# Stage edges of a two-block transformer kernel: other bank pairs, later loads, an unrolled pass, sums on two engines, recurrence steps moved

## The reference, cut to what matters

```python
# first block
y = jnp.einsum('bsmc,mcd->bsmd', branches, w_branch)          # three branches
x = x + jnp.sum(sigmoid(merge_gate) * y, axis=2) @ w_out
h = rms_norm(x, norm_mlp)
x = x + jnp.square(jax.nn.relu(h @ w_mlp_in)) @ w_mlp_out     # 2048 -> 8192 -> 2048
x = rms_norm(x, norm_final)
# second block
h = rmsnorm(x, norm_mix)                                      # two norms, one behind the other
u, q_in, f_in, i_in, g_in = jnp.split(h @ w_in, splits, axis=-1)
# hgrn2_mixer: S_t = diag(f_t) S_{t-1} + (1 - f_t) outer i_t ; o_t = S_t^T q_t
q = silu(q_in)
log_f = log(lb + (1 - lb) * sigmoid(f_in)); k = 1 - exp(log_f)
o = rmsnorm(o, norm_gain) * silu(g_in)                        # norm per head
```

## Time and profile before

| | |
|---|---|
| median of 3 runs | 2823.69 us (2822.1 to 2824.51) |
| the profiled execution | 2825.74 us, its span 2824.2 us |
| PE busy | 2739.8 us, 97% of the span |
| DVE busy | 1437.3 us, 51% |
| ACT busy | 1166.0 us, 41% |
| mean granted TensorE clock | 0.997 of full speed |

### The profile page before, as it was taken

The page is one execution under the profiler, slowest core; times in us unless marked ns, Lnnn a source line. Parts: engine busy times, 40 slices in busy tenths (PEclk is TensorE's granted clock), DMA queues, the critical chain, the costliest instruction groups (busy, mean ns, idle before and its releaser), DMA issues.

```text
span 2824.2 us, 33252 instructions
## 1 busy us (share of the span) xinstructions
PE 2739.8 (97%) x12784; PEld 2077.4 (74%) x12784; DVE 1437.3 (51%) x1645; ACT 1166.0 (41%) x1520; POOL 12.9 (0%) x20
## 2 busy tenths in 40 slices
PE   8999999999999999999999999999999999999896
PEld 6888777778888888888888788888888785434342
DVE  4444455656655565555556744577654463312122
ACT  4443355653354444444444644455444441000001
POOL 0000000000000000000000000000000000000000
PEclk9999999999999999999999999999999999999999
DMA  6966845556656555555555476554555459999997
GB/s 244 329 215 211 300 155 171 180 198 242 214 180 230 186 193 188 185 191 192 186 186 179 171 278 212 191 190 171 209 189 188 158 185 371 426 427 426 427 427 323
DMA packets 115679, 672.57 MB, mean 238 GB/s; under 512 B 12125, under 2 KB 17677, under 8 KB 40688
## 3 DMA queue, kind: packets, MB, share of 16 engines
q1 hardware_dynamic: 86048, 612.52, 59.2%
q10 hardware_dynamic: 27264, 46.58, 4.6%
q0 software_dynamic: 2256, 11.95, 1.2%
HBM read 647.37 MB, written 28.35 MB: 239 GB/s over the span
## 4 chain that ended last, share of the span: by engine, by line
PE 85%; DMA 6%; DVE 4%; ACT 2%; issue 1%; DVEq 1%; ACTq 0%; SPq 0%
PE PS L315 23%; PE PS L317 23%; PE PS L316 23%; PE PS L2123 8%; DMA WIDE<-in_w_down 2%; DMA WIDE<-in_w_up 2%; DMA WIDE<-in_w_gate 2%; PE PS L339 1%; DVE LO L273 1%; PE PS L2021 1%; PE PS L2289 1%; ACT HI L271 1%; PE PS L1477 1%; PE PS L938 0%; PE PS L1630 0%
## 5 line engine op out<-in xcount | busy, mean ns | idle before, releaser
L273 DVE TENSOR_TENSOR LO<-RAW,HI 128x1024 fp32r<-128x1024 f32 x760 | 922.6, 1223 | 832.7 <-ACT HI L271 828.6
L315 PE MATMUL PS<-HI,XH 128*128 128x512 f32 x3040 | 1208.1, 397 | 19.8 <-DVE LO L273 12.2
L317 PE MATMUL PS<-HI,XL 128*128 128x512 f32 x3040 | 1187.0, 390 | 0.0
L316 PE MATMUL PS<-LO,XH 128*128 128x512 f32 x3040 | 1185.7, 390 | 0.0
L271 ACT ACTIVATE HI<-RAW 128x1024 fp32r<-128x1024 f32 x760 | 793.9, 1057 | 783.4 <-PE PS L317 696.6
L315 PEld LDWEIGHTS PS<-HI,XH 128*128 128x128 f32 x3040 | 572.6, 188 | 145.9 <-DVE LO L273 17.0
L317 PEld LDWEIGHTS PS<-HI,XL 128*128 128x128 f32 x3040 | 572.0, 188 | 121.2
L316 PEld LDWEIGHTS PS<-LO,XH 128*128 128x128 f32 x3040 | 573.0, 188 | 118.0 <-issue 2.9
L2123 PE MATMUL PS<-WIDE,XS 128*64 128x512 f32 x1024 | 229.0, 596 | 22.7 <-DMA WIDE<-in_w_up 14.4
L2123 PEld LDWEIGHTS PS<-WIDE,XS 128*64 128x64 f32 x1024 | 75.0, 137 | 160.9 <-issue 160.4
L2123 PE MATMUL PS<-WIDE,Y 128*64 128x512 f32 x496 | 113.0, 598 | 7.9 <-ACT Y L2178 5.5
(11 more groups left out here) (400 smaller groups left out, 1353.6 us busy)
## 6 DMA issues: line engine op xcount, KB each, us to landing
RAW<-in_w_in SPq DMA_DIRECT2D x132, 1024.0 KB, 4.9
RAW<-in_w_mlp_in SPq DMA_DIRECT2D x64, 1024.0 KB, 4.8
RAW<-in_w_mlp_out SPq DMA_DIRECT2D x64, 1024.0 KB, 4.8
WIDE<-in_w_gate SPq DMA_DIRECT2D x64, 1024.0 KB, 23.1
WIDE<-in_w_up SPq DMA_DIRECT2D x64, 1024.0 KB, 18.6
WIDE<-in_w_down SPq DMA_DIRECT2D x64, 1024.0 KB, 21.1
RAW<-in_w_out SPq DMA_DIRECT2D x32, 1024.0 KB, 4.9
RAW<-in_xattn_wkv SPq DMA_DIRECT2D x32, 1024.0 KB, 4.9
```

The costliest lines, as they stand in the source:

```text
L273: dve.tensor_tensor(r["lo"][:, hl, :], r["raw"](k), r["hi"][:, hl, :].bitcast(F32), ALU.subtract).then_inc(lo_done, 1)
L315: pe.matmul(o, xh, wh, start=kt == 0, stop=False)
L316: pe.matmul(o, xh, wl, start=False, stop=False)
L317: mm = pe.matmul(o, xl, wh, start=False, stop=kt == kn - 1)
```

## The change

1. Gate rows: the three loads of a merge column group, and the waits ahead of them, are issued from the hook behind block 0 of its first gemm, behind the split of block 3; before, they stood ahead of the gemm. 2. Bank pairs: the w_out stage uses pairs 1, 0, 1, 0 (`odd=1`) and waits for pair 2 only at its first transposes (in both stages that use `project_add`); the first MLP unit uses pair 1. 3. The loop has 14 passes, and the last pass is written out behind it: in it the last hidden unit is transposed in the middle of the down projection of the one before, to slots 4 to 7. 4. Sums: `both_squares` takes token half 0 on ACT and half 1 on DVE. 5. Recurrence: QQ is made behind AA; the maximum, the KK products and the logarithm move to block 2, the scans to block 3; `factors(1)` moves from block 8 to block 7. 6. The multiplication by the head gain runs while ACT takes the square root (`meanwhile`). Some drains are added (`factors_of_x`, `both_squares`) and one is dropped (`out_gate`). The plan of weight tiles is regrouped for the 14 + 1 passes; its order and its bytes stay as they are.

```diff
-        def rstd(sums, out_, v, n, width):
+        def rstd(sums, out_, v, n, width, meanwhile=None):
...
             t = A(act.activation(out_, out_, ACT.Sqrt))
+            if meanwhile:
+                meanwhile()
             dve.wait_ge(s_act.h, t)
...
             dve.wait_ge(s_act.h, s_act.now())
+            dve.drain()
             dve.tensor_reduce(ss, SMALL[:, 448:448 + 4 * n].rearrange("p (w c) -> p w c", c=4), AX.X, ALU.add)
...
-        all_stored()
-        act.wait_ge(s_lo.h, state["third"])
         pe.wait_ge(a_done.h, 6)
...
             for cc in range(2):
-                act.wait_ge(s_dve.h, s_dve.now())
-                for m in range(3):
-                    ld[2].inc(act.dma_start(GS[:, m, :].rearrange("p (h n) -> p h n", h=2),
-                                            cols_of(SGATE, it * 1024 + (m * D + cc * 512))), 16)
-                gl = ld[2].now()
+                def gate_rows():
+
+                    if it + cc == 0:
+                        all_stored()
+                        act.wait_ge(s_lo.h, state["third"])
+                    act.wait_ge(s_dve.h, s_dve.now())
+                    for m in range(3):
+                        ld[2].inc(act.dma_start(GS[:, m, :].rearrange("p (h n) -> p h n", h=2),
+                                                cols_of(SGATE, it * 1024 + (m * D + cc * 512))), 16)
+
...
-                    r = s.gemm(4, (16, 24, 0)[m], m, hooks={1: lambda c=c: merged_T(c - 1)} if m == 0 and c in (1, 2) else {})
+                    hk = {0: gate_rows} if m == 0 else {}
+                    if m == 0 and c in (1, 2):
+                        hk[1] = lambda c=c: merged_T(c - 1)
+                    r = s.gemm(4, (16, 24, 0)[m], m, hooks=hk)
...
-        def project_add(kt0, ready, hooks, to, gain):
+        def project_add(kt0, ready, hooks, to, gain, odd=0):
...
             def x_T(c):
 
+                if c == 0:
+                    pe.wait_ge(ev[2].h, ev[2].now())
                 chunk_T(X, c, to, gain, (4, 5), x_done[c], x_ready)
 
-            pe.wait_ge(ev[2].h, ev[2].now())
...
-                pair = c % 2
+                pair = (c + odd) % 2
...
-        relu_square(s.gemm(8, 16, 0, **first))
+        relu_square(s.gemm(8, 16, 1, **first), 1)
         s.end()
-        with loop(15, {"ev0": 1, "ev1": 2, "ev2": 2, "s_act": 1, "s_tp": 2, "s_hi": 2, "s_lo": 2}) as it:
+        with loop(14, {"ev0": 1, "ev1": 2, "ev2": 2, "s_act": 1, "s_tp": 2, "s_hi": 2, "s_lo": 2}) as it:
...
-        state["down"] = at["b"] + HL_SLOTS
-        hidden_T(s_act.now())
+        s = Stage()
+        state["down"] = s.base + HL_SLOTS
+        before = s_act.now()
+        relu_square(s.gemm(8, 16, 0, hooks={2: lambda: hidden_T(before)}))
+        last = s_act.now()
+        down(s, hooks={1: {1: lambda: hidden_T(last, 4)}})
+        s.end()
...
+            dve.drain()
             for w, v in enumerate((X, Y3)):
-                for h in range(NH):
-                    ins = act.activation(squares[:, w, h, :], v[:, h, t], ACT.Square, accum_out=SUMS[:, w, h, c:c + 1])
+                ins = act.activation(squares[:, w, 0, :], v[:, 0, t], ACT.Square, accum_out=SUMS[:, w, 0, c:c + 1])
+                dve.tensor_tensor_reduce(squares[:, w, 1, :], v[:, 1, t], v[:, 1, t], 1.0, 0.0, ALU.mult, ALU.add, SUMS[:, w, 1, c:c + 1])
...
-        down(s, hooks={2: {1: lambda: y_T(0)}, 3: {1: lambda: y_T(1)}}, after=gain_chunk)
+        down(s, kt0=4, hooks={2: {1: lambda: y_T(0)}, 3: {1: lambda: y_T(1)}}, after=gain_chunk)
...
             def forget():
                 dve.wait_ge(s_act.h, s_act.now())
-                V(dve.tensor_tensor(QQ, q_ps, EE[0], ALU.mult))
                 for i in range(4):
                     c = slice(i * S, (i + 1) * S)
                     lb, lb1 = (v[:, bass.ds(g * 4 + i, 1)] for v in (LB, LB1))
-                    dve.tensor_scalar(KK[:, c], KK[:, c], lb1, None, ALU.mult)
                     dve.tensor_scalar(AA[:, c], AA[:, c], lb1, lb, ALU.mult, ALU.add)
+                V(dve.tensor_tensor(QQ, q_ps, EE[0], ALU.mult))
+
+            def log_forget():
                 dve.drain()
                 V(dve.tensor_scalar(AA, AA, 1e-19, None, ALU.max))
+                for i in range(4):
+                    c = slice(i * S, (i + 1) * S)
+                    dve.tensor_scalar(KK[:, c], KK[:, c], LB1[:, g * 4 + i:g * 4 + i + 1], None, ALU.mult)
+                act.wait_ge(s_dve.h, s_dve.now())
+                exp_done["log"] = A(act.activation(EE[0], AA, ACT.Ln))
 
             def log_sum():
-                act.wait_ge(s_dve.h, s_dve.now())
-                dve.wait_ge(s_act.h, A(act.activation(EE[0], AA, ACT.Ln)))
+                dve.wait_ge(s_act.h, exp_done["log"])
...
-                rstd(HS, HR, HV, P, 8)
+                e8 = EE[0].rearrange("p (i n) -> p i n", i=8)
+                rstd(HS, HR, HV, P, 8, lambda: dve.tensor_tensor(e8, e8, HG.unsqueeze(1).to_broadcast([P, 8, P]), ALU.mult))
...
-                dve.tensor_tensor(e8, e8, HG.unsqueeze(1).to_broadcast([P, 8, P]), ALU.mult)
-                dve.drain()
...
-            steps = {0: [transposes, loads], 1: [forget], 2: [log_sum], 4: [lambda: exps_of(0)]}
-            level_steps = {4: [lambda: exps_of(0)], 6: [lambda: factors(0)], 7: [lambda: exps_of(1)],
-                           8: [lambda: products(0), lambda: factors(1)], 9: [lambda: exps_of(2), lambda: masked(0)],
+            steps = {0: [transposes, loads], 1: [forget], 2: [log_forget], 3: [log_sum], 4: [lambda: exps_of(0)]}
+            level_steps = {4: [lambda: exps_of(0)], 6: [lambda: factors(0)], 7: [lambda: exps_of(1), lambda: factors(1)],
+                           8: [lambda: products(0)], 9: [lambda: exps_of(2), lambda: masked(0)],
...
-    plan.append((15, unit("w_mlp_in", 1, 1) + rows("w_mlp_out", 0, 16)))
+    plan.append((14, unit("w_mlp_in", 1, 1) + rows("w_mlp_out", 0, 16)))
+    plan.append((1, unit("w_mlp_in", 15) + rows("w_mlp_out", 14, 16)))
```

More of the change, by code:

```diff
@@ L396, in scale, with rsqrt @@
             return (s_act.h, a_), (s_dve.h, v_)
-        def rstd(sums, out_, v, n, width):
+        def rstd(sums, out_, v, n, width, meanwhile=None):
             dve.tensor_scalar(v, sums, 1.0 / n, EPS, ALU.mult, ALU.add)
             dve.drain()
-            rsqrt(out_, v, width)
-        def rsqrt(out_, v, width):
+            rsqrt(out_, v, width, meanwhile)
+        def rsqrt(out_, v, width, meanwhile=None):
             t = V(dve.reciprocal(out_, v))
@@ L1108, in build @@
                     c = 2 * it + cc
-                    r = s.gemm(4, (16, 24, 0)[m], m, hooks={1: lambda c=c: merged_T(c - 1)} if m == 0 and c in (1, 2) else {})
+                    hk = {0: gate_rows} if m == 0 else {}
+                    if m == 0 and c in (1, 2):
+                        hk[1] = lambda c=c: merged_T(c - 1)
+                    r = s.gemm(4, (16, 24, 0)[m], m, hooks=hk)
                     dve.wait_ge(pe_done, r)
-                    dve.wait_ge(ld[2].h, gl)
+                    dve.wait_ge(ld[2].h, ld[2].now())
                     y = Y3[:, :, it * 1024 + cc * 512:it * 1024 + cc * 512 + 512]
@@ L1145, in build @@
         act.wait_ge(s_dve.h, s_dve.now())
-        first = project_add(lambda kt: (kt + 8) % 16, merged_ready, {0: lambda: merged_T(2), 2: lambda: merged_T(3)}, 16, GAIN[:, 1, :])
+        first = project_add(lambda kt: (kt + 8) % 16, merged_ready, {0: lambda: merged_T(2), 2: lambda: merged_T(3)}, 16, GAIN[:, 1, :], odd=1)
         def down(s, pairs=(1, 2, 1, 2), kt0=0, hooks={}, after=None):
@@ L1158, in build, with relu_square @@
         SG = work("sg", 1024, 1024)
-        def relu_square(r):
+        def relu_square(r, pair=0):
             act.wait_ge(pe_done, r)
@@ L1163, in relu_square, with hidden_T @@
             for h in range(NH):
-                ins = act.activation(SG[:, h * W512:(h + 1) * W512], PS[:, h, :], ACT.Relu, scale=R1ST[:, h:h + 1])
-            act.wait_ge(ev[0].h, ev[0].inc(ins))
+                ins = act.activation(SG[:, h * W512:(h + 1) * W512], PS[:, 2 * pair + h, :], ACT.Relu, scale=R1ST[:, h:h + 1])
+            act.wait_ge(ev[pair].h, ev[pair].inc(ins))
             return A(act.activation(HB[:, :, :].rearrange("p h n -> p (h n)"), SG, ACT.Square))
-        def hidden_T(t):
+        def hidden_T(t, kt0=0):
             pe.wait_ge(s_act.h, t)
@@ L1172, in hidden_T @@
             act.wait_ge(pe_done, down_done())
-            state["hidden"] = transpose_split(HB, 4, 0, banks=(6, 7))
+            state["hidden"] = transpose_split(HB, 4, kt0, banks=(6, 7))
         def down_done():
```

## The result

| | median | runs |
|---|---|---|
| before | 2823.03 us (2822.1 to 2827.78) | 7 |
| after | 2812.23 us (2810.98 to 2814.3) | 7 |

The ratio is 0.9958, its 95% interval 0.9948 to 0.9967: the change takes 10.8 us off. The forecast was 2813.6, with a range of 2809.8 to 2818.4. The profiled execution of after took 2811.12 us, its span is 2809.7.

A forecast was written before the change was run, and what follows sets the result against it. The prediction took TensorE, busy 97% of the span, as the bound. Edges 6.4, sums 3.2, recurrence -0.3 and output norm 0.8 made 10.1 us off the 2823.69 us median: 2813.6 us, range 2809.8 to 2818.4.

The forecast's parts named there:

- What bounds the kernel: Whole kernel: TensorE is busy 97% of the span, so almost everything won or lost is its idle time.
- The edges: Stage edges: four PE stops vanish, gate rows 1.20, bank pairs 1.59 and 1.63, unrolled MLP pass 1.98; 6.40 us.
- Bracket plus 0.27: PE's stops at stage edges: each costs its bracketed idle time plus 0.27 us.
- Sums: First w_in_2 gemm: squares shared by ACT and DVE remove PE stops at block 11 and later; 3.2 us, low end 0.
- the cap of 3.36: Squares on two engines: at most 2.37 + 0.99 = 3.36 us for the two PE stops.
- Recurrence: Recurrence steps: block 6's stop won, block 8 delayed, products(1) no longer waits; net -0.3 us for two groups, ends -2.1 and +3.4.
- The rival of a plain reading: Recurrence: gains are as the waits suggest, 3.4 us in place of -0.3, giving 2809.9 us; chance 0.13.
- Output norm: Output norm: gain multiply leaves the chain to the transposes; 0.4 to 0.45 us earlier a group, 0.8 for two.
- The 0.15 beside the 1.29: Output norm: one step of 1.29 + 0.15 us leaves the chain to the transposes.
- the bound of the first w_in_2 unit: First w_in_2 unit: DVE becomes its bound, sums gain 2.0 us or less; 2815 to 2818 us with a recurrence delay; chance 0.22.
- the expert stage kept the lead: Expert stage: the rival had it, bound by weight traffic, give the gain back, leaving 2823.7 us; chance 0.03.
- repeated the stop at block 8: Recurrence: the rival had DVE take over and block 8's 1.6 us stop recur at six later levels; about 2835 us; chance 0.03.

The follow-up runs named there:

- The old order: Changed kernel with the recurrence's forget and log_sum steps as before the change, factors(1) still one hook early; median 2811.46 us.
- a kernel with the key products rightly placed: Changed kernel with forget and log_sum steps as before, and the four KK products right behind the first exponents' subtractions; median 2809.2 us.
- the kernel with the old edges: Changed kernel with gate rows issued before the first merge gemm, pair 2's wait ahead of the first w_out gemm, and pairs 0, 1, 0, 1; 2816.54 us, one run.

## Why the prediction was right, step by step

- **What bounds the kernel.** That nearly all is won or lost in idle time of PE, one stop at a time, held: the steps of the lead add up to 11.25 us, each at the place where the earlier trace rows had a wait, and undoing three of them together gave their plain sum.
- **The edges: 6.40 forecast, 6.51 measured** (1.22 + 1.62 + 1.67 + 2.00). Bracket plus 0.27 was the right price of a stop. One sentence of that part failed: the gate loads were to land no later than before. They went out at the same moment (627.46 - 2.88 = 624.58 us, as in after), but the third took 8.37 us to land instead of 6.47. That cost after's profile nothing, because three blocks of lead hid it, but two of the ten profiles with a joint semaphore lost 1.4 us there.
- **Sums: 3.2 forecast, 3.61 measured.** DVE's squares took 0.69 us and started 0.61 apart, where 0.7 was taken, and DVE kept pace. The two stops were worth 2.37 and 1.02 us, where 2.37 and 0.99 were priced. The term was undersized because I took 3.2 below the cap of 3.36 on a doubt that had no ground, and because the block behind the second stop gave 0.22 more, which the sum did not have.
- **Recurrence: -0.3 forecast, -0.02 measured.** In group 1 the steps are 0.99 us won at block 6, 0.44 and 1.60 lost at blocks 7 and 8 (so block 8 is 1.0 later than before, where 1.1 was forecast), 0.94 paid back by factors(1) and 0.12 in small steps: the mechanism in all three parts. The old order shows that the spreading by itself loses 1.0 us a group. The rival of a plain reading, +3.4, fell for after, although a kernel with the key products rightly placed got it and more (4.2).
- **Output norm: 0.8 forecast, 1.15 measured**, and 1.14 when undone. The step that failed is "the four small operations then start 1.0 us later": they start 0.72 later. The 0.15 beside the 1.29 failed too, since it counts the fence twice; it hid half of the first error.
- **The other rivals.** DVE was not the bound of the first w_in_2 unit; the expert stage kept the lead (14.13 at the last dense matmul, 14.5 at the end); no later level of the recurrence repeated the stop at block 8.
- **The start point.** I took the sum off the median, not off the profiled execution. The account shows that this was right: 2.88 us of the difference between the two profiles lie ahead of the first edit. The total, 2813.6 against 2812.23, is 1.4 us off. Half of that is the start, a median of 2823.69 from three runs where seven give 2823.03, and half the sum, 10.1 against 10.8; by the steps the sum is 1.1 too small.

## What to carry to other kernels

When two kernels run the same matmuls in the same order, subtract their start times pair by pair: the steps of the difference, read once they have settled, price each edit to 0.1 us where medians blur at 1. Compare whole times only at equal granted clock. Before an operation is moved off a crowded stretch, look for the engine's idle time and put it exactly there; the four key products won 2.2 us in one gap and nothing two blocks later. And when a load is moved, give each consumer its own semaphore, so that the slowest of several transfers doesn't decide for the first.

## What was not expected of the hardware

- Three 512 KB loads, issued together in the midst of the weight stream, took up to 9.1 to 11.4 us to land when issued behind a split, and up to 6.8 or 6.9 when issued ahead of it. After moved 403 GB/s from 628 to 632 us. The traces point to sharing with the weight transfers. In before and in the kernel with the old edges the next 1 MB weight transfer went out 2.94 us behind the third gate load, at all four column groups, and the load took 5.9 to 6.9 us. In after it went out 0.1 to 0.4 us behind it, and the load took 8.1 to 9.3. No run moves that transfer alone.
- Near 45, 290 and 358 us of the kernel's start TensorE fell to its lower clock (a share of 0.5) for 3.41 us, once for 6.83. Of the fourteen profiles six have it at all three places, three at 45 and 358, and five at 358 alone. One such stretch more, at 290, is 1.58 of the 2.80 us by which before's and after's profile differ there.
- A fence between two 1024-wide DVE operations costs 0.16 us, alone and without any dependence.
